# Prompt attention in a four-layer decoder step: value operands held as high and low parts side by side

## The reference

```python
s_c = jnp.einsum('bqghd,bcgd->bghqc', q, kc).astype(f32) * ATTN_SCALE
p_c = masked_softmax(s_c, c_end[None, :] <= q_pos[:, None])
o_c = jnp.einsum('bghqc,bcgd->bqghd', p_c.astype(vc.dtype), vc)
...
o_s = jnp.einsum('bghqk,bgqkd->bqghd', p_s.astype(v_sel.dtype), v_sel)
...
o_w = jnp.einsum('bghqw,bwgd->bqghd', p_w.astype(vw.dtype), vw)
return g[..., 0:1] * o_c + g[..., 1:2] * o_s + g[..., 2:3] * o_w
```

## Time and profile before

| | us |
|---|---|
| median of 3 runs | 1606.05 (1605.51 to 1606.75) |
| profiled execution, its own time | 1605.53 |
| its span in the trace | 1603.9 |
| prompt stage of attention | 163 to 341 |
| sampled tokens | 341 to 374 |
| output projection and the rest | 374 to 1603.9 |

### The profile page before, as it was taken

The page is one execution under the profiler, slowest core; times in us unless marked ns, Lnnn a source line. Parts: engine busy times, 40 slices in busy tenths (PEclk is TensorE's granted clock), DMA queues, the critical chain, the costliest instruction groups (busy, mean ns, idle before and its releaser), DMA issues.

```text
span 1603.9 us, 31366 instructions
## 1 busy us (share of the span) xinstructions
PE 1565.6 (98%) x12506; PEld 1530.5 (95%) x12506; DVE 1004.4 (63%) x1584; ACT 721.6 (45%) x1317; POOL 321.2 (20%) x742
## 2 busy tenths in 40 slices
PE   8999899988999999999999999999999999999999
PEld 8999677868999999999999999999999999999999
DVE  3346787775888445534567787868873455355684
ACT  4445677863454333313434536744443343143352
POOL 4702344520055012202210000002540121022000
PEclk9999999998999999999999999999999999999999
DMA  7736000053222222222232222242222222222312
GB/s 267 149 105 223 1 1 1 11 179 104 67 92 84 96 85 82 90 93 81 91 104 90 74 87 80 83 130 69 91 91 93 80 92 93 80 93 93 104 67 96
DMA packets 42634, 148.00 MB, mean 92 GB/s; under 512 B 6432, under 2 KB 8752, under 8 KB 42176
## 3 DMA queue, kind: packets, MB, share of 16 engines
q1 hardware_dynamic: 36864, 125.58, 24.3%
q0 software_dynamic: 5632, 20.48, 3.8%
HBM read 140.57 MB, written 9.10 MB: 93 GB/s over the span
## 4 chain that ended last, share of the span: by engine, by line
PE 88%; DVE 7%; ACT 3%; issue 2%; DMA 0%; POOL 0%; ACTq 0%; DVEq 0%; SPq 0%
PE PS L2064 77%; PE PS L2229 3%; PE PS L2191 2%; ACT ARENA L850 1%; PE PS L2115 1%; PE PS L2116 1%; DVE SMALL L1372 1%; PE PS L2362 1%; PE PS L2181 1%; DVE LO L474 1%; PE PS L2182 1%; DVE X L1671 1%; PE PS L2215 1%; DMA RAW<-in_w_stream 0%; ACT HI L468 0%
## 5 line engine op out<-in xcount | busy, mean ns | idle before, releaser
L2064 PE MATMUL PS<-XH,HI 128*128 128x272 f32 (+1 forms) x1936 | 406.6, 291 | 9.3 <-DVE XL L1216 8.5
L2064 PE MATMUL PS<-XH,LO 128*128 128x272 f32 (+1 forms) x1936 | 403.0, 289 | 0.0
L2064 PE MATMUL PS<-XL,HI 128*128 128x272 f32 (+1 forms) x1936 | 402.2, 288 | 0.0
L468 ACT ACTIVATE HI<-RAW 128x1024 fp32r<-128x1024 f32 x223 | 235.1, 1057 | 250.4 <-PE PS L2064 227.6
L474 DVE TENSOR_TENSOR LO<-RAW,HI 128x1024 fp32r<-128x1024 f32 x223 | 274.1, 1230 | 102.0 <-ACT HI L468 101.5
L2064 PEld LDWEIGHTS PS<-XH,HI 128*128 128x128 f32 x1936 | 307.0, 189 | 10.6 <-DVE LO L474 8.5
L2064 PE MATMUL PS<-GH,HI 128*128 128x272 f32 (+1 forms) x1504 | 313.6, 290 | 0.8 <-DVE LO L474 0.6
L2064 PE MATMUL PS<-GH,LO 128*128 128x272 f32 (+1 forms) x1504 | 311.0, 288 | 0.0
L2064 PE MATMUL PS<-GL,HI 128*128 128x272 f32 (+1 forms) x1504 | 310.5, 288 | 0.0
L2064 PEld LDWEIGHTS PS<-XL,HI 128*128 128x128 f32 x1936 | 306.0, 189 | 0.1
L2064 PEld LDWEIGHTS PS<-XH,LO 128*128 128x128 f32 x1936 | 304.6, 189 | 0.0
(11 more groups left out here) (383 smaller groups left out, 1886.2 us busy)
## 6 DMA issues: line engine op xcount, KB each, us to landing
RAW<-in_w_stream SPq DMA_DIRECT2D x223, 512.0 KB, 3.3
ARENA<-in_cache_cmp POOLq DMA_DIRECT2D x32, 128.0 KB, 3.0
out_win_old<-in_win_copy POOLq DMA_DIRECT2D x1, 4064.0 KB, 18.3
X<-in_x SPq DMA_DIRECT2D x4, 544.0 KB, 6.9
X<-in_x POOLq DMA_DIRECT2D x1, 2176.0 KB, 8.2
ARENA<-in_cache_sel POOLq DMA_DIRECT2D x16, 128.0 KB, 3.1
ARENA<-in_cache_win POOLq DMA_DIRECT2D x4, 512.0 KB, 5.7
SEL<-in_cache_sel SPq DMA_DIRECT2D x16, 128.0 KB, 2.0
```

What stands on the lines that cost most here:

```text
L468: nc.scalar.activation(HI[:, s * CH:(s + 1) * CH], RAW[:, (c % RAWS) * CH:(c % RAWS + 1) * CH], ACT.Copy).then_inc(hi_ready, 1)
L2064: ins = mm(PS[0:rows, b + h, 0:width], w[:, 0:rows], cols(part, h), start=first and len(parts) == 2 and n == 0, stop=last and len(parts) == 1)
```

## The change

- `VV` in place of `VH` and `VL`: for each source and key block 256 columns lie in the order high part of group 0, low part of group 0, low part of group 1, high part of group 1. The 128 stationary columns for a unit's group are its high and low part together, so one product gives the sums with the high part in the group's 64 partitions and those with the low part in the other 64. `values` issues two products per block (with the high and the low part of the weights) instead of three.
- The low sums have to be added: `out_hi` copies them on ScalarE from the other 64 partitions to SBUF (`low_kept`), and `out_lo` on VectorE adds them after its subtraction, behind a wait for itself and one for the copy.
- Compressed values and weights stay fp32: `cmp_values` issues two fp32 products of 64 stationary columns in place of six fp32r products of 128; their parts `PCH`, `PCL` and the low part of `VCZ` go. The turned compressed weights are copied half by ScalarE and half by VectorE.
- `cmp_values(n)` moves from u % 4 == 3 of its own group into `values(n, 0)`, after the first block, which now opens the sum; the waits for the bank move along. For the last group it comes after the loop.
- `VV` is written in two instructions on each engine instead of one; ScalarE also waits for the DMA that stores the values' source. The clearing of the second mask buffer of the sampled tokens waits for the last compressed product (`vcz_free`), since they share memory.

```diff
-        VH, VL = over("VH", ARENA_AT, at_kt4 + 4096, 1024), over("VL", ARENA_AT, at_kt4 + 1024, 1024)
+        VV = [over("VV0", ARENA_AT, at_kt4 + 4096, 1024), over("VV1", ARENA_AT, at_kt4 + 1024, 1024)]
+        VV4 = [t.rearrange("p (k s c) -> p k s c", k=4, s=4) for t in VV]
...
-        VCZ = over("VCZ", ARENA_AT, at_kt4 + 512, 512)
+        VCZ = KT4[:, 512:768]
...
+        def low_sums(n):
+
+            return PS[64 - 64 * group(n)[2]:128 - 64 * group(n)[2], 6 + n % 2, :].rearrange("p (j t) -> p j t", j=4)
...
-                    s.activation(VH.rearrange("p (h c) -> p h c", h=2), PS[:, 6:8, :], ACT.Copy).then_inc(tr_took, 1)
+                    act.wait_ge(kv_out, 32)
+                    for r in range(2):
+                        ins = s.activation(VV4[r][:, :, 0:4:3, :], PS[:, 6 + r, :].rearrange("p (k g c) -> p k g c", k=4, g=2),
+                                           ACT.Copy)
...
             def cmp_hi_part(c):
                 m = CMP_BLOCK_AT[c]
                 act.wait_ge(pt_done, m + 1)
-                s.activation(PCH[c % 2], PS[:, 4 + m % 2, :], ACT.Copy).then_inc(pt_act, 1)
+                s.activation(PCF[c % 2][:, 0:256], PS[:, 4 + m % 2, 0:256], ACT.Copy).then_inc(pt_act, 1)
 
             def out_hi(n):
                 act.wait_ge(pv_done, n + 1)
                 s.activation(heads_of(XH3, n), sums_of(n), ACT.Copy).then_inc(ot_hi, 1)
+                s.activation(low_kept(n), low_sums(n), ACT.Copy).then_inc(low_copied, 1)
...
-            def compressed_values():
-                dve.wait_ge(w2_took, 2)
-                for r in range(4):
-                    v.tensor_tensor(VCZ[32 * r:32 * r + 32, 256 + 64 * r:320 + 64 * r],
...
-            def cmp_lo_part(c):
+            def cmp_half(c):
                 m = CMP_BLOCK_AT[c]
                 dve.wait_ge(pt_act, m + 1)
-                for jq in range(2):
...
+                v.tensor_copy(PCF[c % 2][:, 256:512], PS[:, 4 + m % 2, 256:512]).then_inc(pt_dve, 1)
 
             def out_lo(n):
                 dve.wait_ge(ot_hi, n + 1)
-                sub_lo(heads_of(XL3, n), sums_of(n), heads_of(XH3, n), ot_lo)
+                chain.did(v.tensor_tensor(heads_of(XL3, n), sums_of(n), heads_of(XH3, n).bitcast(F32), ALU.subtract))
+                chain.sync()
+                dve.wait_ge(low_copied, n + 1)
+                v.tensor_tensor(heads_of(XL3, n), heads_of(XL3, n).bitcast(F32), low_kept(n).bitcast(F32), ALU.add)\
+                    .then_inc(ot_lo, 1)
...
             for x in range(2):
+                if x:
+                    dve.wait_ge(vcz_free, 1)
                 chain.did(v.memset(PMS2[x], 0.0))
...
                 for e in range(2):
-                    for m, (v0, pc) in enumerate(((0, hi), (256, hi), (0, lo))):
-                        mm(at[:, :, e, :], VCZ[:, v0 + P * e:v0 + P * e + P],
-                           pc.rearrange("p (b t) -> p b t", b=2), start=m == 0 and e == 0, stop=False)
+                    ins = mm(at[:, :, e, :], VCZ[:, P * e + r0:P * e + r0 + 64], pc, start=False, stop=False)
+                if n == 15:
+                    ins.then_inc(vcz_free, 1)
...
                 for x in range(lo, hi):
                     r, kt = blocks[x]
-                    vs = slice(r * SEQ + kt * P, r * SEQ + kt * P + P)
-                    for m, (vv, pt) in enumerate(((VH, PTSH[n % 2]), (VL, PTSH[n % 2]), (VH, PTSL[n % 2]))):
-                        ins = mm(at, vv[:, vs], pt[:, r, kt, :], start=False, stop=x == len(blocks) - 1 and m == 2)
+                    both = VV4[r][:, kt, 2 * gg:2 * gg + 2, :].rearrange("p s c -> p (s c)")
+                    for m, pt in enumerate((PTSH[n % 2], PTSL[n % 2])):
+                        ins = mm(at, both, pt[:, r, kt, :], start=x == 0 and m == 0,
+                                 stop=x == len(blocks) - 1 and m == 1)
                 if quarter == 3:
                     ins.then_inc(pv_done, 1)
+                if quarter == 0:
+                    cmp_values(n)
...
                 if u == 1:
-                    pe.wait_ge(qk_lo, 21)
+                    pe.wait_ge(w2_took, 2)
...
-                if u % 4 == 3:
-                    cmp_values(n)
```

More of the change, by code:

```diff
@@ L379, in heads_of, with low_kept @@
             return x[64 * gg:64 * gg + 64, j:j + 4, c0:c0 + P]
+        def low_sums(n):
+            return PS[64 - 64 * group(n)[2]:128 - 64 * group(n)[2], 6 + n % 2, :].rearrange("p (j t) -> p j t", j=4)
+        def low_kept(n):
+            r0 = 64 * group(n)[2]
+            if n % 2 and n > 8:
+                return PTSH[1][r0:r0 + 64, 0, 3, :].rearrange("p (j t) -> p j t", j=4)
+            return heads_of(XL3, n + (3 if n % 2 else 1))
         def side_by_side(dst, u, r):
@@ L803, in _ @@
                     s.activation(GT, PS[:, 5, 64:256], ACT.Copy).then_inc(w2_took, 1)
-                    s.activation(VH.rearrange("p (h c) -> p h c", h=2), PS[:, 6:8, :], ACT.Copy).then_inc(tr_took, 1)
+                    act.wait_ge(kv_out, 32)
+                    for r in range(2):
+                        ins = s.activation(VV4[r][:, :, 0:4:3, :], PS[:, 6 + r, :].rearrange("p (k g c) -> p k g c", k=4, g=2),
+                                           ACT.Copy)
+                        if r == 0:
+                            chain.did(ins)
+                    ins.then_inc(tr_took, 1)
                 if n == 4:
@@ L1340, in _ @@
                     dve.wait_ge(kv_out, 32)
-                    hv = lambda ap: ap.rearrange("p (h c) -> p h c", h=2)
-                    sub_lo(hv(VL), PS[:, 6:8, :], hv(VH), qk_lo)
+                    for r in range(2):
+                        ins = v.tensor_tensor(VV4[r][:, :, 1:3, :], PS[:, 6 + r, :].rearrange("p (k g c) -> p k g c", k=4, g=2),
+                                              VV4[r][:, :, 0:4:3, :].bitcast(F32), ALU.subtract)
+                        if r == 0:
+                            chain.did(ins)
+                    ins.then_inc(qk_lo, 1)
                 if n == 4:
@@ L1353, in _ @@
                     dve.wait_ge(qk_lo, 17)
-                    v.tensor_copy(VCZ, ZERO.to_broadcast([P, 512])).then_inc(vcz_clear, 1)
-            def compressed_values():
-                dve.wait_ge(w2_took, 2)
-                for r in range(4):
-                    v.tensor_tensor(VCZ[32 * r:32 * r + 32, 256 + 64 * r:320 + 64 * r],
-                                    PS[32 * r:32 * r + 32, 5, 64 * (r % 2):64 * (r % 2) + 64],
-                                    VCZ[32 * r:32 * r + 32, 64 * r:64 * r + 64].bitcast(F32), ALU.subtract).then_inc(qk_lo, 1)
+                    v.memset(VCZ, 0.0).then_inc(vcz_clear, 1)
             g0 = GT[:, 0:48].rearrange("p (h r) -> p h r", r=3)[:, :, 0:1]
```

31 lines of the change are left out of this document (14 added, 17 removed).

## The result

The changed kernel took 1616.22 us (median of 4 runs, 1613.89 to 1618.25), the kernel before 1606.4 beside it (4 runs, 1605.51 to 1606.97): a ratio of 1.0061, 95% interval 1.0049 to 1.0074. It is slower, by 9.8 us. The forecast had the direction, but the time lies above its 1610.3 and above its range, which ended at 1614.0. The profiled execution was the shortest of the four, 1613.89, with a span of 1612.3 against 1603.9.

What follows compares the result with a forecast made beforehand. A closed VectorE-ScalarE loop, about as long as TensorE's work, was taken as the bound. +10.8 - 1.1 - 0.4 - 2.6 - 1.0 - 0.9 = +4.8 us on 1605.53 gave 1610.3, range 1605.0 to 1614.0.

Steps and rivals of the forecast that it cites:

- The loop without a gap: Prompt stage: VectorE's maximum, ScalarE's exponentials, VectorE's reciprocal, next maximum bound it, 1.84 or 2.32 us a unit; chance 0.57.
- Low sums: VectorE's addition delays the next maximum by 0.72 us at 14 group boundaries in the loop: +10.1 us.
- TensorE's gates: In the loop, a shorter TensorE removes the maximum's waits for scores: -2.6 us, bounds 0 and -2.6.
- turned weights: ScalarE's waits for turned weights, 22.9 us, lie mostly in the maximum's shade: -1.0 us, bounds 0 and -3.
- halved copies: ScalarE's copies of compressed weights shrink from 0.60 to some 0.40, exponentials following at two of four places: -0.4 us.
- TensorE's own work falls by about 14 us: On TensorE, 80 products fewer save 18.5 us; compressed products at 0.95 instead of 0.72 a group add 4.
- Start and end of the loop: Start without `VCZ`'s low part: -1.1 us; end, with one product less and compressed products behind sampled scores: -0.9.
- Tail: Last group's addition (n = 15), between ScalarE's copy of the sums and the sampled tokens' copies: +0.72 us.
- The clock: Rival: TensorE's granted clock falls four more times in the loop, adding 4 us: 1614.3; chance 0.12.
- TensorE as the bound: Rival: TensorE bounds the prompt stage after all, so its shorter work makes the kernel faster: 1596; chance 0.11.
- the hidden addition: Rival: VectorE's idle time absorbs the addition at half the boundaries or more, 10.1 becoming 5 or less: 1605.3; chance 0.20.
- 0.57 x 0.85 + 0.12: Chance of slower by over 0.2%: own forecast 0.57, about 0.85 of it over 1609.3, plus the clock's 0.12.

Runs made afterwards that it cites:

- the kernel before with the sums moved: Kernel before, ScalarE's copy of the sums moved behind the exponentials and VectorE's subtraction ahead of the next unit's reciprocal: 1606.06 us, ratio 0.9998.
- the product alone: Kernel before without the product of the values' low part (80 products fewer), nothing else changed: 1603.82 us against 1606.5, ratio 0.998.
- the addition alone: Kernel before with only a second VectorE operation of the addition's shape behind the subtraction of the sums: 1616.95 us against 1606.5, ratio 1.007.
- the first profile: Profiled execution of the changed kernel's first timing: 1613.89 us, span 1612.3, mean clock 0.994.
- the first session: First timing of the changed kernel, unedited, four executions beside the kernel before: median 1616.22 us, ratio 1.0061.
- the third session: Changed kernel timed a third time, unedited, five executions, beside the run with repeated products: median 1618.24 us against 1605.54, ratio 1.0071.
- its compressed values side by side: Changed kernel with compressed values as high and low parts in fp32r, four products a group instead of two fp32 ones: 1618.6 us, ratio 1.0079.
- The run with the late sums: Changed kernel, sums' copy behind the exponentials, subtraction and addition (low sums read from PSUM) each ahead of a reciprocal: 1603.82 us, ratio 0.9982.
- repeated products: Changed kernel with the first product of the scores made twice for units 0 to 31 (48 products more): 1615.43 us, ratio 1.0059.

## Why the prediction was wrong in the number and right in the sign

The time is 5.9 us above the forecast. Of these, 3.6 are terms of the sum that came out otherwise in the profiled execution, the low sums first, and 2.3 are what the median lies above that execution. Either part alone would have left the time within the range.

**What bounds the kernel: right.** The loop without a gap was the bound for anything added to VectorE (+10.4 alone) and the chain that named only TensorE was not to be taken for it (-2.7 for 18.5 us of work). That both are about equally long was stated, and the kernel before with the sums moved (no gain, and TensorE waited for in its place) bears it out.

**Low sums: mechanism right, the term mis-sized; this is the step of the sum that failed most.** "+0.72 a group; the bounds are 0.6 and 0.9": seven of 14 boundaries have 0.72 to 0.75 and three 0.8, but two have 1.16 and 1.21 and two 0.95. I had priced the addition as if VectorE worked alone; that GpSimd scales weights just behind the reciprocal, at the place where the addition falls, was in the trace. 11.8 instead of 10.1: +1.7. The two sizes behind the 0.72 were each about 0.11 short (with an addition that is not held up, the next maximum starts 1.45 after the subtraction and not 1.33, without one 0.72 and not 0.61); that the difference is right all the same is luck.

**TensorE's gates, turned weights, halved copies: -4.0 forecast, -3.1 measured.** The gates are confirmed (-2.4 with the product alone). What failed is "TensorE's own work falls by about 14 us", taken to make the compressed products free: they cost 1.2 us a group instead of the 0.95 taken, so that it falls by 11, and alone they lose 1.0 us of the loop. Against this stand the 1.5 us that the addition alone gives back, which the sum did not have. +0.9 by the first profile; by the others (3.4 and 1.4 given back) +0.6 and +2.6.

**Start and end of the loop: right.** -1.2 for -1.1, -0.9 for -0.9; ScalarE's second copy was free, as forecast.

**Tail: +0.7 forecast, +2.1 measured.** In the 14 profiles of the experiments it varies from 23.0 to 25.0 us between the same two points, with and without an addition; the kernel before had 22.54, the least of all. The one addition took its 0.72; where the other 1.4 comes from stays open. The granted clock does not explain it: in the changed kernel it was 0.69 to 0.88 in four stretches between 364 and 380, but in the kernel before 0.64, 0.93 and 0.58 in three between 360 and 372, which makes some 6.8 us at 1.2 GHz in both.

```profile
360.00:364.00 4.00, 3.60 (x98) 3.36 (x98) 3.08 (x12) 3.98 (x12) 0.00 (x0) 0.64 0.02 4
364.00:368.00 4.00, 1.60 (x13) 1.17 (x11) 2.97 (x7) 0.60 (x1) 0.00 (x0) 0.93 0.57 158
368.00:372.00 4.00, 4.00 (x143) 3.33 (x145) 3.44 (x9) 1.82 (x3) 0.00 (x0) 0.58 0.28 109
```

**The clock: I held it for a rival of 0.12 and priced a fall at 1 us, "at most 1.4"; in the sum it stood at nothing.** The terms so far, 1.7 + 0.9 + 1.4, with -0.4 since the stage began earlier, -0.1 at its start and +0.1 behind the start of the output projection, make 3.6: the span's +8.4 instead of +4.8. The median of the first session lies 2.3 over that execution. In the third session a difference of that kind goes with the clock; in the first it does so for one execution (0.988) and not for the other (1616.1 at 0.993), and none of them was profiled, so that the 2.3 are put down to the clock and not shown to be its price. The price itself was wrong twice. The row was misread, since the 0.91 of its first stretch belongs to the same fall: (0.09 + 0.34) x 4 makes 1.7 at most and not 1.4. And I took every fall to be as long as that one. A short fall cost the loop 0.3 us, less than I took, one of 6.8 us 2.1, and the changed kernel with its compressed values side by side has one of some 10 us, for 2.5. The run with the late sums has another of that length:

```profile
228.00:232.00 4.00, 2.08 (x18) 1.79 (x16) 3.33 (x6) 3.95 (x9) 1.58 (x3) 0.99 0.01 4
232.00:236.00 4.00, 3.71 (x16) 3.41 (x16) 3.87 (x10) 2.23 (x8) 1.93 (x4) 0.50 0.00 0
236.00:240.00 4.00, 4.00 (x17) 3.47 (x16) 2.18 (x7) 1.76 (x10) 1.24 (x2) 0.50 0.00 0
240.00:244.00 4.00, 4.00 (x15) 2.37 (x15) 1.66 (x5) 1.18 (x6) 0.88 (x2) 0.73 0.00 0
```

From its maximum at 227.40 to that at 242.87 it took 15.5 us. The kernel before with the same move, at the full clock there, took 11.9 for the same units (230.29 to 242.19), so this fall cost at most 3.6 us. The kernel before without the move (10.6) is not the measure for it, as the move by itself makes these units longer.

Where TensorE is the bound, a short fall costs more: behind the start of the output projection the first profile takes 1229.2 us with a clock of 0.57 in 384 to 388, that of the third session 1227.7 with 1.00.

```profile
384.00:388.00 4.00, 4.00 (x22) 4.00 (x21) 0.00 (x0) 0.00 (x0) 0.63 (x2) 0.57 0.68 238
```

```profile
384.00:388.00 4.00, 4.00 (x34) 4.00 (x33) 0.00 (x0) 0.00 (x0) 0.10 (x1) 1.00 0.65 238
```

At a mean clock of 0.995 the changed kernel has spans of 1610.2, 1612.4 and 1612.7, which is 6.3 to 7.8 us over the middle of the kernel before in the same session. What the +7.7 to +12.7 of the three sessions have beyond that goes with the clock in the third. What makes one execution fall deeper than the next at the same place stays open.

**The rivals.** TensorE as the bound is refuted, the hidden addition too: no boundary absorbed it. The clock came on top of the forecast instead of in its place. By the terms written down, the chance of a slower kernel is 0.57 x 0.85 + 0.12 = 0.60 and not 0.61, which changes nothing.

## What to carry to other kernels

Where two loops are equally long, taking work from one gives only its waits, and a small operation put on the other costs its full length nearly every time (11.8 us at the boundaries, of which 1.5 came back): first find a place in the shade of a wait for what is added, then count the saving. With additions on VectorE ask what GpSimd does at that moment, and let one input come from PSUM. And when TensorE is relieved in a stage where its clock falls already, put longer falls into the range, not only more of them, and time more than one execution: the profiled one may be the shortest.

## What the runs showed of the hardware that was not expected

- An addition with both inputs in SBUF ended 0.53 us after GpSimd's running scaling, for up to 1.17 in place of 0.69; with one input in PSUM 16 of 16 took 0.683 to 0.694. Where both started together, it was the scaling that took longer (1.27 in place of 0.77).
- Two fp32 products of 64 stationary columns between fp32r products cost 1.2 us, with an idle time of 0.35 to 0.39 of the weight load on either side:

```profile
287.39 0.62 PEld L2225 LDWEIGHTS PS<-ARENA 128*64 128x64 f32 x4 [0.35 <-issue]
288.40 0.19 PEld L2196 LDWEIGHTS PS<-KKH,GL 128*128 128x128 f32 x1 [0.39 <-issue]
```

- Nine us of repeated products for TensorE put all five executions at a mean clock of 0.995 or 0.996, where 10 of 13 without them were lower, and did not lengthen the median beyond the noise (1615.43 against 1614.19 and 1618.24).
- What a fall of the granted clock costs depends on its length and on what waits for TensorE: in the loop 0.3 us for 3.4 us at 1.2 GHz, 2.1 for 6.8, 2.5 and at most 3.6 for some 10; in the output projection, which TensorE bounds, 1.5 for 3.4.
